# Three steps instead of two for each weight block that a hybrid decoder prepares for its next stage

## The reference

```python
mod = silu(c) @ w_ada + b_ada                       # six vectors of 1024 a sequence
h = rms_norm(x, norm1_w) * (1 + sc1) + sh1
proj = h @ w_in                                     # retention q,k,v,gate | mLSTM q,k,v,gate | 2x4 gates
y_r = head_norm(retention(rotary(rq), rotary(rk), rv)) * silu(rg)      # 4 heads of 128, chunks of 128
y_m = head_norm(mlstm(silu(conv4(mq, mk)), mv, mi, mf)) * sigmoid(mo)  # 4 heads of 128, chunks of 128
x = x + g1 * (concat(y_r, y_m) @ w_out)
h2 = rms_norm(x, norm2_w) * (1 + sc2) + sh2
u, val = split(h2 @ w_up);  u = conv3(u)
x = x + g2 * ((silu(u) * val) @ w_down)             # then a last rms_norm; all states are returned
```

## Time and profile before

| | |
|---|---|
| median of 3 runs | 2828.12 us (2827.47 to 2828.34) |
| profiled execution, its own time | 2829.14 us |
| its span | 2827.3 us |
| TensorE matmul busy | 2513.2 us (89%) |
| VectorE busy | 1674.8 us (59%) |
| ScalarE busy | 838.0 us (30%) |
| GpSimd busy | 400.3 us (14%) |
| mean granted TensorE clock | 0.939 of full |

### The profile page before, as it was taken

One profiled execution on the slowest core, in us unless ns is written; L12 is line 12 of the kernel. 1 busy time (PEld: TensorE's weight loads), 2 busy tenths in 40 slices (PEclk: granted clock), 3 DMA queues, 4 the chain that ended last, 5 costly groups with the idle time before them and its releaser, 6 DMA issues. The chain is left out here.

```text
span 2827.3 us, 45028 instructions
## 1 busy us (share of the span) xinstructions
PE 2513.2 (89%) x17415; PEld 1552.9 (55%) x17415; DVE 1674.8 (59%) x3330; ACT 838.0 (30%) x1273; POOL 400.3 (14%) x385
## 2 busy tenths in 40 slices
PE   2688889969897999769959999999999978999998
PEld 0345445547676777635536666666666643444444
DVE  6445554445777786648857777777777755222222
ACT  2333333303443444224432222222322224111110
POOL 0112223310000000002231222221222200000000
PEclk6799999979999999779979999999999988999999
DMA  9325541153133320153312122222122217232321
GB/s 249 102 100 170 162 159 74 52 172 125 50 110 115 142 90 21 35 169 131 128 51 68 52 75 70 75 75 71 57 66 75 70 64 259 78 99 72 104 70 47
DMA packets 194606, 279.51 MB, mean 99 GB/s; under 512 B 16296, under 2 KB 131544, under 8 KB 192332
## 3 DMA queue, kind: packets, MB, share of 16 engines
q1 hardware_dynamic: 194517, 278.34, 31.3%
HBM read 203.02 MB, written 75.29 MB: 98 GB/s over the span
## 5 line engine op out<-in xcount | busy, mean ns | idle before, releaser
L324 PE MATMUL d_po<-d_w,d_a_parts 128*128 128x512 f16 x704 | 268.8, 382 | 28.2 <-DVE d_w L2853 27.5
L325 PE MATMUL d_po<-d_w,d_a_parts 128*128 128x512 f16 x704 | 268.7, 382 | 0.0
L326 PE MATMUL d_po<-d_w,d_a_parts 128*128 128x512 f16 x704 | 268.4, 381 | 0.0
L2377 PE MATMUL py<-h_parts,wide_weights 128*128 128x384 f16 (+1 forms) x792 | 246.4, 311 | 17.9 <-DVE u_p L2513 17.9
L2378 PE MATMUL py<-h_parts,wide_weights 128*128 128x384 f16 (+1 forms) x792 | 246.2, 311 | 0.0
L2379 PE MATMUL py<-h_parts,wide_weights 128*128 128x384 f16 (+1 forms) x792 | 246.2, 311 | 0.0
L324 PE MATMUL prj<-w_heads,h_parts_t 128*128 128x512 f16 x512 | 196.1, 383 | 10.8 <-DVE h_parts_t L941 5.4
L325 PE MATMUL prj<-w_heads,h_parts_t 128*128 128x512 f16 x512 | 195.8, 382 | 0.0
L326 PE MATMUL prj<-w_heads,h_parts_t 128*128 128x512 f16 x512 | 195.6, 382 | 0.0
L2840 DVE SCALAR_TENSOR_TENSOR d_out<-d_po,d_scale,g_p 128x1024 f32<-128x1024 f32 x16 | 20.5, 1283 | 287.2 <-PE d_po L326 287.2
L324 PE MATMUL m_prj<-m_h,w_heads 128*128 128x128 f16 (+1 forms) x1088 | 179.6, 218 | 12.1 <-DMA m_h<-h_parts 10.8
(11 more groups left out here) (455 smaller groups left out, 5667.5 us busy)
## 6 DMA issues: line engine op xcount, KB each, us to landing
C_new<-in_w_up_dram SPq DMA_DIRECT2D x11, 2048.0 KB, 7.7
u_raw<-in_w_up_dram SPq DMA_DIRECT2D x44, 512.0 KB, 5.6
d_a<-act_cols SPq DMA_DIRECT2D x15, 1408.0 KB, 7.4
act_cols<-u_a SPq DMA_DIRECT2D x44, 384.0 KB, 2.4
win_raw<-in_w_in_dram SPq DMA_DIRECT2D x8, 2048.0 KB, 15.8
win_raw<-in_w_ada_dram SPq DMA_DIRECT2D x8, 2048.0 KB
u_wd<-in_w_down_dram SPq DMA_DIRECT2D x22, 512.0 KB, 4.0
d_raw<-in_w_down_dram SPq DMA_DIRECT2D x11, 1024.0 KB, 6.9
```

What stands on the lines that cost most here:

```text
L324: nc.tensor.matmul(out, left[0], right[0], start=(k == 0), stop=False)
L325: nc.tensor.matmul(out, left[0], right[1], start=False, stop=False)
L326: return nc.tensor.matmul(out, left[1], right[0], start=False, stop=last)
L2377: nc.tensor.matmul(out, left[0], right[0], start=(start and k == 0), stop=False, skip_group_check=True)
```

## The change

`find_scale` is split into `find_max` and `set_scale`, and a block takes three steps: the maximum in the first, the scale in the second, both cuts in the third. In `phase_ret` these are the steps 3b+2, 3b+3 and 3b+4. GpSimd's `reduce` moves to step 3b+3, and there from the end of the step to a place between `sin_part` and `head_rstd`. The late parts, two to a block as before, are carried by steps 3b+2 and 3b+3, so the steps 2, 3, 5, 6, 8, 9, 11 and 12; steps 4, 7, 10 and 13 have none. SyncE's stores and loads follow: a block is stored and the next one loaded after step 3b+4. The loops of all engines now hold three steps and run four times (three on TensorE, two on SyncE, with the rest written out). In `phase_mls` the three parts are in steps 4b+2, 4b+3 and 4b+4; `reduce`, the loads and the stores stay where they were.

```diff
-    def find_scale(self, dve, b):
-        steps = Steps(dve, self.steps, 6 * b)
+    def find_max(self, dve, b):
         dve.wait_ge(self.landed, 16 * b + 16)
         self.nc.vector.tensor_reduce(self.red[:, 0:1], self.raw[:], AX.XY, ALU.max, apply_absolute_value=True).then_inc(self.maxed, 1)
+
+    def set_scale(self, dve, b):
+        steps = Steps(dve, self.steps, 6 * b)
         dve.wait_ge(self.all_maxed, b + 1)
         power_of_two(self.nc, steps, self.red[:, 1:2], self.red[:, 2:3], self.red[:, 3:4], self.bits[:])
...
             with sp.Fori(1, LATE // 2 - 1) as b:
-                step(2 * b + 2)
+                step(3 * b + 2)
                 save_late(2 * b, 0)
                 load_late(2 * b + 1, 1)
-                step(2 * b + 3)
+                step(3 * b + 3)
                 save_late(2 * b + 1, 1)
                 load_late(2 * b + 2, 0)
+                step(3 * b + 4)
                 prep.store_parts(sp, b)
                 prep.load_raw(sp, b + 1)
...
-            with pe.Fori(1, LATE) as p:
-                step(p + 2, P, P, P, p, p)
-            with pe.Fori(LATE + 2, NCH - 1) as c:
-                step(c, P, P, P, None, LATE)
+            step(3, P, P, P, 1, 1)
+            step(4, P, P, P, None, 2)
+            with pe.Fori(1, LATE // 2) as b:
+                step(3 * b + 2, P, P, P, 2 * b, 2 * b)
+                step(3 * b + 3, P, P, P, 2 * b + 1, 2 * b + 1)
+                step(3 * b + 4, P, P, P, None, 2 * b + 2)
+            step(NCH - 2, P, P, P, None, LATE)
             step(NCH - 1, P, P, NS)
...
-            with act.Fori(1, 4) as b:
-                step(2 * b + 2, P, P, P, P, qs_p)
-                step(2 * b + 3, P, P, P, P, qs_p, lambda: prep.cut_hi(act, b))
...
+            with act.Fori(0, 4) as b:
+                step(3 * b + 2, P, P, P, P, qs_p)
+                step(3 * b + 3, P, P, P, P, qs_p)
+                step(3 * b + 4, P, P, P, P, qs_p, lambda: prep.cut_hi(act, b))
...
-                step(2 * b + 2, P, P, P, P, steps, mask_p, lambda: prep.find_scale(dve, b), (2 * b, 0))
-                step(2 * b + 3, P, P, P, P, steps, mask_p, lambda: prep.cut_lo(dve, b), (2 * b + 1, 1))
...
+                step(3 * b + 2, P, P, P, P, steps, mask_p, lambda: prep.find_max(dve, b), (2 * b, 0))
+                step(3 * b + 3, P, P, P, P, steps, mask_p, lambda: prep.set_scale(dve, b), (2 * b + 1, 1))
+                step(3 * b + 4, P, P, P, P, steps, mask_p, lambda: prep.cut_lo(dve, b))
...
             def step(c, T, Ta, Tnn, dec, between=None):
                 sin_part(c, T)
+                if between:
+                    between()
                 head_rstd(c - 1, Ta)
                 decay_k(c, T, dec)
                 gate_weight(c, T)
                 if Tnn:
                     norm.rms(pool, c + 2, Tnn)
-                if between:
-                    between()
...
             with pool.Fori(0, 4) as b:
-                step(2 * b + 2, P, P, P, dec_p, lambda: prep.reduce(pool, b))
-                step(2 * b + 3, P, P, P, dec_p)
...
+                step(3 * b + 2, P, P, P, dec_p)
+                step(3 * b + 3, P, P, P, dec_p, lambda: prep.reduce(pool, b))
+                step(3 * b + 4, P, P, P, dec_p)
...
@@ phase_mls, ScalarE @@
-                step(4 * b + 3, P, P, lambda: prep.cut_hi(act, b))
-                step(4 * b + 4, P, P)
+                step(4 * b + 3, P, P)
+                step(4 * b + 4, P, P, lambda: prep.cut_hi(act, b))
...
@@ phase_mls, VectorE @@
-                step(4 * b + 2, P, P, steps, lambda: prep.find_scale(dve, b))
+                step(4 * b + 2, P, P, steps, lambda: prep.find_max(dve, b))
                 find_max(4 * b)
-                step(4 * b + 3, P, P, steps, lambda: prep.cut_lo(dve, b))
+                step(4 * b + 3, P, P, steps, lambda: prep.set_scale(dve, b))
                 find_max(4 * b + 1)
-                step(4 * b + 4, P, P, steps)
+                step(4 * b + 4, P, P, steps, lambda: prep.cut_lo(dve, b))
                 find_max(4 * b + 2)
```

More of the change, by code:

```diff
@@ L662, in _ @@
             load_late(2, 0)
+            step(4)
             prep.store_parts(sp, 0)
@@ L665, in _ @@
             with sp.Fori(1, LATE // 2 - 1) as b:
-                step(2 * b + 2)
+                step(3 * b + 2)
                 save_late(2 * b, 0)
                 load_late(2 * b + 1, 1)
-                step(2 * b + 3)
+                step(3 * b + 3)
                 save_late(2 * b + 1, 1)
                 load_late(2 * b + 2, 0)
+                step(3 * b + 4)
                 prep.store_parts(sp, b)
                 prep.load_raw(sp, b + 1)
-            step(LATE)
+            step(NCH - 5)
             save_late(LATE - 2, 0)
             load_late(LATE - 1, 1)
-            step(LATE + 1)
+            step(NCH - 4)
             save_late(LATE - 1, 1)
+            step(NCH - 3)
             prep.store_parts(sp, 3)
-            with sp.Fori(LATE + 2, NCH - 2) as c:
-                step(c)
             load_rope(NCH - 1, P, (NCH - 1) * P)
@@ L915, in _ @@
             step(1, P, P, P, P, qs_p)
-            step(2, P, P, P, P, qs_p)
-            step(3, P, P, P, P, qs_p, lambda: prep.cut_hi(act, 0))
-            with act.Fori(1, 4) as b:
-                step(2 * b + 2, P, P, P, P, qs_p)
-                step(2 * b + 3, P, P, P, P, qs_p, lambda: prep.cut_hi(act, b))
-            step(10, P, P, P, P, qs_p)
-            with act.Fori(11, NCH - 2) as c:
-                step(c, P, P, P, P, qs_p)
+            with act.Fori(0, 4) as b:
+                step(3 * b + 2, P, P, P, P, qs_p)
+                step(3 * b + 3, P, P, P, P, qs_p)
+                step(3 * b + 4, P, P, P, P, qs_p, lambda: prep.cut_hi(act, b))
             step(NCH - 2, P, P, P, NS, qs_p)
@@ L1039, in _ @@
             with dve.Fori(0, 4) as b:
-                steps = Steps(dve, s["steps"], base.n + per + 2 * b * (per + more))
-                step(2 * b + 2, P, P, P, P, steps, mask_p, lambda: prep.find_scale(dve, b), (2 * b, 0))
-                step(2 * b + 3, P, P, P, P, steps, mask_p, lambda: prep.cut_lo(dve, b), (2 * b + 1, 1))
-            with dve.Fori(10, NCH - 2) as c:
-                steps = Steps(dve, s["steps"], base.n + (c - 1) * per + LATE * more)
-                step(c, P, P, P, P, steps, mask_p)
-                assert steps.n == per
+                steps = Steps(dve, s["steps"], base.n + per + b * (3 * per + 2 * more))
+                step(3 * b + 2, P, P, P, P, steps, mask_p, lambda: prep.find_max(dve, b), (2 * b, 0))
+                step(3 * b + 3, P, P, P, P, steps, mask_p, lambda: prep.set_scale(dve, b), (2 * b + 1, 1))
+                step(3 * b + 4, P, P, P, P, steps, mask_p, lambda: prep.cut_lo(dve, b))
             steps = Steps(dve, s["steps"], base.n + (NCH - 3) * per + LATE * more)
@@ L1118, in _ @@
             with pool.Fori(0, 4) as b:
-                step(2 * b + 2, P, P, P, dec_p, lambda: prep.reduce(pool, b))
-                step(2 * b + 3, P, P, P, dec_p)
-            with pool.Fori(10, NCH - 2) as c:
-                step(c, P, P, P, dec_p)
+                step(3 * b + 2, P, P, P, dec_p)
+                step(3 * b + 3, P, P, P, dec_p, lambda: prep.reduce(pool, b))
+                step(3 * b + 4, P, P, P, dec_p)
             step(NCH - 2, P, P, NS, dec_p)
```

## The result

| | before | after |
|---|---|---|
| median of 4 runs each, side by side | 2827.80 us | 2766.24 us (2763.07 to 2768.43) |
| ratio, 95% interval | | 0.978 (0.976 to 0.980) |
| profiled execution, its own time | 2829.14 us | 2768.43 us |
| its span | 2827.3 us | 2766.7 us |
| mean granted TensorE clock | 0.939 | 0.951 |

The change gains 61.6 us (2.2%) where 55.9 us were forecast (2772.2 us). The time lies in the range of 2765 to 2787 us, near its lower end.

The account below looks back on a forecast made before the run. TensorE bounds the retention phase, VectorE's chain the mLSTM steps with a block. Gains of 42.6 (46.4 - 2.8 - 1.0) and 13.3 us from 2829.14 give 2773.2, so a median of 2772.2 us; range 2765 to 2787 us, chance 0.85.

Parts of the forecast that it names:

- GpSimd's hold of 13.6 us: Retention phase: reduce holds GpSimd from request at 193.14 to sin_part at 206.77, for 0.56 us of instructions.
- The excess of 46.4 us: Retention steps 3 to 10: 268.31 us against 221.9 undisturbed; the waits ahead of outputs and slow matmuls would all go.
- 2.8 and 1.0: Retention phase costs: turn_x waits 0.35 us after all eight late parts, +2.8; second loads of pairs just landing, +1.0 us.
- The tight cover: Retention step 3b+3: the reduce's hold ends 1.8 to 3.6 us before head_rstd is wanted, so hidden, cost 0.
- The row of the hold with a long idle stretch: A measured idle stretch of 13.54 us instead of 7.21 behind a partition maximum; with it the hold ends 2.8 us late.
- rival 1: Retention phase: the reduce is late for head_rstd, full price 11 us, giving 2783 us; chance 0.09.
- What was costed at nothing: Retention phase: reduce, seven small operations, cut_lo, cut_hi, SyncE's queue and longer loop bodies, each put at 0.
- my two bounds: Retention phase: two sine operations take 2.5 us, or 6.5 us beside other VectorE work.
- the lower bound: mLSTM phase: a third pause costs 0.7 us of slow matmuls too, so the gain is 11.9 us.
- Rival 2: Retention phase: a pair's second late load meets a block's transfers, 9 us late four times, 2808 us; chance 0.05.
- Rival 3: Retention wait stays, its cause misread, 2815 us, chance 0.03; or the maximum's wait moves to set_scale, 2828 us, chance 0.03.
- Rival 4: Both phases: the reduce holds VectorE too; with all 13.6 us it costs 70, giving 2843 us; chance 0.04.

Follow-up runs that it names:

- kernel 3: Kernel after the change, but GpSimd's reduce again last in its step 3b+3: 2808.08 us, ratio 0.993 to the kernel before.
- kernel 4: Kernel after the change, but GpSimd's reduce ahead of the sine part of step 3b+3: 2809.42 us, ratio 0.994 to the kernel before.
- kernel 10: Kernel before the change, with only GpSimd's reduce moved between sine part and head_rstd of step 2b+3: 2792.03 us, ratio 0.987.
- kernel 6: Kernel after the change, with four useless 128x512 multiplications behind each retention-phase reduce on GpSimd: 2779.28 us, ratio 0.983 to the kernel before.
- kernel 9: kernel 3 with each late w_ada load cut to its first eighth, so part of the modulation uses old values: 2794.65 us, one run.
- kernel 7: Kernel after the change, but two steps a block in the retention phase, both cuts in the second: 2771.34 us, ratio 0.980 to the kernel before.

## Why the prediction was right, step by step

- **The bound and the idle stretch.** The claim that the wait ahead of `outputs` was GpSimd's hold of 13.6 us, in two halves, holds. Kernels 3 and 4 bring the waits back by moving the reduce and nothing else, kernel 10 takes nearly all of them away in the same manner, and kernel 6 shows the second half ending at 206.62, 7.14 us behind the partition maximum.
- **The excess of 46.4 us goes** less 2.8 and 1.0: forecast 42.6, measured 41.4. The eight waits of `turn_x` were 3.1 us for 2.8. The wait for a late part's data (1.0) did not appear. Seven steps with a late part and five without would take 7 x 27.98 + 5 x 26.06 = 326.2 us; 331.1 were measured, 4.9 us more, where 3.8 were forecast. Of these 3.2 are waits, and 1.7 are busy time in the steps that have one (28.20 us of PE instead of 27.98, 26.22 instead of 26.06), a term that the sum lacked.
- **The tight cover.** The margin was put at 1.8 to 3.6 us and measured at 2.4 to 3.5. The row of the hold with a long idle stretch was rightly a warning, though of another thing than I used it for. I left it open what made it long; it lay beside a DMA share of 1.00, and kernels 3 and 9 show for the first stretch that this is what counts. In the changed kernel the DMA share is 0.04 to 0.20 over the four first stretches, which are 5.65 to 6.04 us, and 0.19 in the 7 us behind the first block's partition maximum. So what speaks against rival 1 is when the transfers run, which the prediction did not look at; its price is real, and was put too low at 1:1. Kernel 6, some 1 to 1.6 us late a block, lost 10.8 us in steps 3 to 14, so 2.8 us late would have cost more than the 11 us.
- **What was costed at nothing** was nothing. The sine part took 1.44 + 1.27 us, near the lower of my two bounds, and the rotation, `cut_hi`, the seven operations and SyncE's queue leave no row in which TensorE waits for them.
- **mLSTM phase.** Forecast 13.3 us and steps of 33.8, 30.8 and 33.9; measured 13.5 and 33.70, 30.80 and 33.72 (second block 34.26, 30.80 and 34.41 in this trace, 33.75, 30.80 and 33.72 in another). By the three steps of a block together the gain was 7.0 to 7.1 us in three cases and 5.8 in one (before 105.2 us; after 98.2 and 99.5 here, 98.1 and 98.3 in the other), where 6.67 were forecast. That the sum of 13.5 came within 0.2 us of the forecast is so in part luck. A third pause did cost its 0.7 us of busy time, as the lower bound had it: PE is busy 29.98, 29.98 and 30.12 us in the three steps, against 29.99, 30.10 and 29.32. But to call them slow matmuls was wrong: the middle one of the three, 29.98 us busy, has a mean clock of 1.00. What the bound missed is that the waiting fell by more than 6.67 us, 7.6 in the first block, by the same rows; why, no run asked.
- **The sum** was 55.9, the changed code gave 54.9 and the medians 61.6. The term missing from it is no part of the change: a step at a low clock that the profiled execution of before had and that of after had not, 2.6 us behind the mLSTM phase, whose code is the same in both, and scatter of about 3 us either way. On another chip the same pair stood 59.7 us apart.
- **Rival 2** (transfers in each other's way) had the right mechanism and the wrong place: with three steps there is no such wait, with two (kernel 7) the load of x comes late, in a trace that is 4.6 us longer. **Rival 3** is excluded by the trace. **Rival 4** (VectorE held too) is excluded: beside the first stretch, from 193.2 us on, VectorE's operations took 0.69, 0.68 and 0.69 us, as the same ones did before.

On the first stretch the Trainium skill (GPSIMD Engine Reference, 2.1 Instruction dispatch) gives about 6 us. The traces agree in the retention phase where the DMA share over the stretch is at most 0.32 (5.65 to 6.47 us), and disagree beside a whole 2 MB load (8.91 to 10.43 us); there the measurement decides.

## What to carry to other kernels

A short library call on GpSimd is priced by the time from its request to GpSimd's next ordinary instruction, and by what is queued behind it, not by its own duration. Ask for each place in the engine's program who waits next for that engine; here moving one call behind the next sine part was worth 37 of 41 us, and taking away the visible wait at most the rest. Before adding to such a cover, measure the margin with a few useless instructions: past it each microsecond cost more than one here.

## What the runs showed of the hardware that was not expected

- In the retention phase the idle stretch ahead of the partition maximum is 5.7 to 6.5 us and grows to 8.9 to 10.4 us when a 2 MB load starts with it (not when one ends in its first 2 us); it shrinks back when the load is cut to an eighth. The second stretch, hidden or 6.7 to 7.7 us elsewhere, was 11.5 to 14.2 us beside DMA shares of 0.87 to 1.01. That both are themselves transfers is what this suggests; no run shows it directly, and the second was not tried.
- VectorE and GpSimd slow each other by pairs of operations, and by very different amounts. A sine operation that lies wholly beside the one-input maximum takes 1.27 us, as alone (188.82 us in the timeline of after). In kernel 7 it meets the two-input `cut_lo`, and both suffer, GpSimd by a factor of four (a row of each engine's timeline):

```profile
219.42 5.45 POOL L1092 TENSOR_TENSOR rot_sin<-qk_raw_t,rope_t 128x512 f32<-128x512 f32 x1
```

```profile
218.23 5.51 DVE L324 SCALAR_TENSOR_TENSOR mlsw_cut<-win_raw,mlsw_red,mlsw_cut 128x4096 f16<-128x4096 f32 x1
```

  The ends say more than the lengths: `cut_lo` ends at 223.74, 1.03 us longer than its 4.48, and the sine operation 1.13 us behind it, at 224.87. So nearly all of its work may have been done after `cut_lo` was over; these rows fit a wait for the other engine, and no run tests it.

- TensorE's clock: four waits of 1.1 to 1.5 us (kernel 10) left the mean of steps 3 to 14 at 1.00; four of 5.0 to 5.7 us (kernel 9) brought it to 0.97, and those of 5.0 to 9.8 us (kernel 3) to 0.95. Between these the length alone does not tell: single waits of 2.29, 3.05 and 2.42 us (kernel 6) left their steps at 1.00, while one of 2.43 us (kernel 7) and one of 2.69 us (kernel 6) went with 0.95 and 0.94.
